# A two-layer encoder trunk with a mixture of experts on one core: gathering the tokens of two experts at once, the gate addition ahead of the routing, and another last combine

## The chip, the cores and the metric

The kernel runs on one core of a Trainium2 chip. TensorE (PE) multiplies, VectorE (DVE) and ScalarE (ACT) do the elementwise work, GpSimd (POOL) builds constants and issues a few DMAs, SyncE (SP) issues the weight DMAs. The metric is the device time of one launch in microseconds (us), the median of several runs.

## What is computed

Two layers over 256 tokens of width 1024, all in float32. Each layer normalizes, mixes along the sequence in four head groups and adds a gated residual; then comes a feed-forward part: a dense SwiGLU in layer 0, a top-2-of-8 mixture of SwiGLU experts in layer 1. A last RMSNorm ends it. The change lies in the mixture and behind it.

```python
D_MODEL, SEQ, DEPTH, D_FF, N_EXPERTS, TOP_K = 1024, 256, 2, 3584, 8, 2

def swiglu(h, w1, w3, w2):
    return (jax.nn.silu(h @ w1) * (h @ w3)) @ w2

def moe_ffn(h, router_w, router_b, w1, w3, w2):
    logits = h @ router_w + router_b
    top_v, top_i = lax.top_k(logits, TOP_K)
    combine = sum over k of one_hot(top_i) * softmax(top_v)
    y = jnp.zeros_like(h)
    for e in range(N_EXPERTS):
        y = y + combine[..., e:e + 1] * swiglu(h, w1[e], w3[e], w2[e])
    return y

h = modulate(rms_norm(x, norm_ffn[1]), sh2, sc2)
x = x + g2[:, None, :] * moe_ffn(h, ...)
return rms_norm(x, norm_final)
```

## The kernel before

Tokens lie in two tiles (`tt`) of 128 partitions. Each expert has 128 slots; its tokens are gathered into them by a product with a 0/1 matrix. `routing` computes logits on PE, picks the two best experts per token on DVE, and counts positions on PE; `dispatch_of` (L1706) writes `dispatch[token, slot]` for one expert, with one compare per token tile. `gather` (L1086) multiplies the normalized rows `xn` with it, in plain float32: 8 feature blocks of 128 by 2 token tiles, 128 columns each, 16 products an expert, which the trace records as 32. ACT copies the eight blocks out of PSUM with shift and scale (`fill_two`, L2095, into `x_slots`) and rounds them to `x_high` (`fill_high`); DVE subtracts for `x_low` (`fill_low`).

An expert reads 21 chunks of weights of 2 MB through a ring of six, in `MOE_ORDER`. Each chunk is two units. For each unit ACT rounds the weights to float32r (`w_high`, three buffers, L2121), DVE subtracts for the rest (`ring_low`, L1727), and PE does high x high, high x low and low x high (L1117 to L1119): 12 products of 512 columns. So ACT works three units ahead of PE at most (`used_at(r, m - HIGHS)`), and DVE behind ACT. In `two_experts` of ACT and DVE the place of every other step is written by hand behind a unit `m` of 42. PE's order is in `one_expert`: the next expert's gather stands between the units of `up(2, "w1")` and `up(2, "w3")`, that is ahead of unit 24. The result of an expert is gated (`y_gate`), split, spread back over the tokens by `combine` (8 products) and added to x (`sums`) in the course of the next expert; the last one's behind the loop. At the end `final` normalizes: ACT squares and takes roots, DVE divides and multiplies (L1841), SP stores.

A DMA that POOL issues loads the gate's bias row (L626) once the old one has been used; `gate(1, 1, ...)` adds two row sums to it on DVE (L1371), behind the routing. The number of tokens of the fullest expert, `most_i`, is loaded into a register by ACT and DVE ahead of their first steps for the experts (L2282, L1911); a second pass over the experts runs only where it is over 128, and the profiled execution has none.

The lines that the wait of the gate hangs on:

```python
            def gate(l, which, b):
                rep = 2 * l + which
                eng.wait_ge(s_gate, 16 * (rep + 1))
                eng.wait_ge(gate_t.sem, gate_t.at("sum", rep))
```

Of the kernel before, what the change touches and what calls it, by code (L numbers as in the profile page):

```python
# [6 lines left out]
P = 128  # L7
D = 1024
KB = D // P
T = 256  # L10
# [94 lines left out]
class Steps:  # L105
# [11 lines left out]
    def said(self, name):  # L117
# [86 lines left out]
        ("d0 d1").split(),  # L204
    "choice_v":
        ("c").split(),
# [5 lines left out]
        ("g0 g1").split(),  # L212
# [13 lines left out]
        ("la lb").split(),  # L226
    "fill_a":
        ("x0 x1 x2 x3 h0 x4 x5 x6 x7 h1").split(),
# [3 lines left out]
        ("y").split(),  # L232
    "end_v":
        ("rc0 o00 o01 rc1 o10 o11").split(),
    "end_a":
        ("table sq00 b0 sq10 b1 sq01 rt0 sq11 rt1").split(),
# [3 lines left out]
def hybrid_stream_block(nc, a, out):  # L240

    ctx = ExitStack()
    with ctx:
# [73 lines left out]
        x_slots = mb("x_slots", [P, KB, SLOTS])  # L317
# [3 lines left out]
        dispatch = mb("dispatch", [P, 2, TT, SLOTS])  # L321
        choice = mb("choice", [P, 2, 3, TT])
        chosen = mb("chosen", [P, 3, NE + 1, TT])
# [6 lines left out]
        y_high = mb("y_high", [P, D], F32R)  # L330
        y_low = mb("y_low", [P, D], F32R)
# [42 lines left out]
        disp_v, choice_v = steps("disp_v"), steps("choice_v")  # L374
        slot_v, slot_a, gather_t = steps("slot_v"), steps("slot_a"), steps("gather_t")
# [3 lines left out]
        end_v, end_a, half_t = steps("end_v"), steps("end_a"), steps("half_t")  # L379

# [144 lines left out]
        def last_sum(rep):  # L525

            return combined(rep, expert(rep, 0, NE))

        def combined(q, r):

            return r - 1 + q
# [15 lines left out]
        def _(eng):  # L547
# [44 lines left out]
            def store(rep):  # L592

                for tt, half in ((0, None), (1, 0), (1, 1)):
                    c = slice(0, D) if half is None else slice(half * W, (half + 1) * W)
                    eng.wait_ge(end_v.sem, end_v.at(f"o{tt}{1 if half is None else half}", rep))
                    eng.dma_start(out[0, tt * P:(tt + 1) * P, c], out_place(tt)[:, c]).then_inc(s_out, 16)
# [14 lines left out]
        def _(eng):  # L612
# [83 lines left out]
            for g, win in enumerate(WINDOWS):  # L696
# [29 lines left out]
               .then_inc(s_final, 16)  # L726

# [4 lines left out]
        def _(eng):  # L732
# [353 lines left out]
            def gather(b, u, first, name):  # L1086
# [5 lines left out]
                mark(ins.then_inc(gather_t.sem, 1), gather_t, name)  # L1092

            def experts(q):
                eng.wait_ge(disp_v.sem, disp_v.at("d1", q * NE))
                gather(bank[4], 0, 0, "g0")
                gather(bank[5], 0, 4, "g1")
# [11 lines left out]
                combine(combined(q, expert(q, 0, NE)))  # L1109

            def one_expert(q, g, u):
                r = expert(q, g, u)
                old = combined(q, r)
# [7 lines left out]
                def up(J, name, first, middle=None):  # L1121
# [4 lines left out]
                    for half in range(n_j):  # L1126
                        if half and middle:
                            middle()
                        if J == 0 and name == "w1":
                            eng.wait_ge(fill_v.sem, fill_v.at("lb" if half else "la", r))  # L1130
# [59 lines left out]
                def spread_turn():  # L1190
# [3 lines left out]
                    for tt in range(TT):  # L1194
                        ins = nc.tensor.transpose(bank[7][:, tt * P:(tt + 1) * P], dispatch[:, u, tt, :], ident)
# [26 lines left out]
                if not is_last(q, g, u):  # L1222
                    eng.wait_ge(disp_v.sem, disp_v.at("d1", r + 1))
                    eng.wait_ge(moe_v.sem, moe_v.at("al2", r))
                    gather(bank[6], (u + 1) % 2, 0, "g0")
                    eng.wait_ge(moe_v.sem, moe_v.at("al3", r))
                    gather(bank[7], (u + 1) % 2, 4, "g1")
                up(2, "w3", 2)
                down(2)
                down(3)  # L1230

                if is_last(q, g, u):
                    eng.wait_ge(moe_v.sem, moe_v.at("al3", r))
                else:
                    eng.wait_ge(fill_a.sem, fill_a.at("x3", r + 1))
                turn(4)
                if not is_last(q, g, u):
                    eng.wait_ge(fill_a.sem, fill_a.at("x7", r + 1))
# [12 lines left out]
            def combine(rep):  # L1251

                for tt, half, b in COMBINE:
# [4 lines left out]
                    if tt == 0:  # L1258
                        eng.wait_ge(comb_v.sem, comb_v.at(f"yl{half}", rep))
                    mark(mm(bank[b][:, :], spread[:, tt * P:(tt + 1) * P], y_low[:, half * W:(half + 1) * W],  # L1260
                            start=False, stop=True).then_inc(comb_t.sem, 1), comb_t, f"c{tt}{half}")

# [50 lines left out]
        def _(eng):  # L1313
# [336 lines left out]
            def routing():  # L1650
# [5 lines left out]
                ids = iota_f[:, 0:NE].unsqueeze(1).to_broadcast([P, TT, NE])  # L1656
                eng.wait_ge(route_t.sem, route_t.at("rows"))
# [24 lines left out]
                dispatch_of(0, 0, 0)  # L1682
# [13 lines left out]
                done_(nc.vector.memset(chosen[:, :, NE, :], 0.0).then_inc(route_v.sem, 1), "idle")  # L1696
                gate(1, 1, (bank[0], bank[1]))

            def fill_low(part, rep, u):

                eng.wait_ge(fill_a.sem, fill_a.at(f"h{part}", rep))
                k = 4 * part
                done(eng, tt_(x_low[:, u, k:k + 4, :], x_slots[:, k:k + 4, :], x_high[:, u, k:k + 4, :].bitcast(F32),
                              ALU.subtract).then_inc(fill_v.sem, 1), fill_v, "lb" if part else "la", rep)

            def dispatch_of(e, u, rep):  # L1706

                for tt in range(TT):
                    done(eng, ts_(dispatch[:, u, tt, :], iota_f, chosen[:, 0, e, tt:tt + 1],
                                  chosen[:, 1, e, tt:tt + 1], ALU.is_equal, ALU.mult).then_inc(disp_v.sem, 1),  # L1710
                         disp_v, f"d{tt}", rep)

            def dispatch_again(e, u, rep):
# [601 lines left out]
```

## Time and profile before

| | |
|---|---|
| median of 3 runs | 1590.28 us (1589.90 to 1591.51) |
| the profiled execution's own time | 1590.84 us |
| its span, first to last instruction | 1589.0 us |
| mean granted clock of TensorE | 0.988 of full speed |
| busy: PE, DVE, ACT | 98%, 82%, 62% |
| gathers, first and last start | 568.01 us, 1398.10 us |
| first expert's first product | 574.05 us |
| last store issued | 1584.68 us and 1.12 us for two |

The busy shares are of the whole span. The experts fill it from 574 us on. Ends of PE's instructions are modelled, so that neighbours overlap in the rows; the time that a product takes from the next is read from start to start.

### The profile page before, as it was taken

What the parts mean: (1) busy time and instruction counts of PE and PEld (TensorE: products, weight loads), DVE (VectorE), ACT (ScalarE), POOL (GpSimd) and SP (SyncE); (2) the same over time, 40 slices, a digit from 0 to 9 for tenths busy, and PEclk for the clock granted to TensorE, in tenths of its full rate; (3) what the DMA queues carried; (4) which work ended last, traced back from release to release, by engine and by line L of the source; (5) the groups of instructions that cost most, each with busy time, mean ns of one, the idle gap of its engine ahead of it and who ended that gap; (6) DMA issues with size and microseconds to landing.
All of it is one profiled execution on the core that took longest, in us unless ns stands there. A gap on an engine that the chain in (4) does not pass through costs nothing.

```text
span 1589.0 us, 19707 instructions
## 1 busy us (share of the span) xinstructions
PE 1560.7 (98%) x8037; PEld 1280.9 (81%) x8037; DVE 1308.5 (82%) x1185; ACT 978.7 (62%) x879; POOL 43.5 (3%) x116
## 2 busy tenths in 40 slices
PE   8999999999999989999999999999999999999997
PEld 6886789999888468888888888888888888888885
DVE  5888878888674559899799799899988989989987
ACT  2432433444444357777777777687787777677775
POOL 5300100000000000000000000000000000000000
PEclk8999999999999999999999999999999999999999
DMA  9845788887823269999999999899999999999990
GB/s 354 309 162 210 265 312 324 308 299 266 304 96 117 79 226 366 339 366 346 336 366 354 329 368 361 322 368 364 354 339 369 341 339 373 344 343 364 346 354 28
DMA packets 157142, 481.05 MB, mean 303 GB/s; under 512 B 4218, under 2 KB 6438, under 8 KB 157046
## 3 DMA queue, kind: packets, MB, share of 16 engines
q1 hardware_dynamic: 155120, 475.02, 80.9%
q0 software_dynamic: 1392, 3.58, 0.7%
q8 instruction: 65, 1.06, 0.3%
q10 hardware_dynamic: 534, 1.13, 0.2%
q14 instruction: 31, 0.25, 0.0%
HBM read 478.66 MB, written 1.05 MB: 302 GB/s over the span
## 4 chain that ended last, share of the span: by engine, by line
PE 92%; DVE 5%; DMA 1%; ACT 1%; issue 1%; DVEq 0%; ACTq 0%
PE bank L1119 20%; PE bank L1117 20%; PE bank L1118 19%; PE bank L813 6%; PE bank L1037 3%; PE bank L1039 3%; PE bank L1038 3%; PE bank L810 3%; PE bank L1090 2%; PE bank L1013 2%; PE bank L1014 2%; PE bank L1148 2%; PE bank L1015 2%; DMA ring<-in_w_mod_dram 1%; PE bank L998 1%; PE bank L747 1%
## 5 line engine op out<-in xcount | busy, mean ns | idle before, releaser
L1727 DVE TENSOR_TENSOR ring_low<-ring,w_high 128x2048 fp32r<-128x2048 f32 x336 | 766.9, 2291 | 116.1 <-ACT w_high L2121 108.8
L2121 ACT ACTIVATE w_high<-ring 128x2048 fp32r<-128x2048 f32 x336 | 646.4, 1924 | 240.7 <-PE bank L1119 230.8
L1117 PE MATMUL bank<-w_high,x_high 128*128 128x512 f32 x896 | 355.9, 397 | 2.2 <-issue 2.2
L1118 PE MATMUL bank<-ring_low,x_high 128*128 128x512 f32 x896 | 355.9, 397 | 0.0
L1119 PE MATMUL bank<-w_high,x_low 128*128 128x512 f32 x896 | 353.9, 395 | 0.0
L1117 PEld LDWEIGHTS bank<-w_high,x_high 128*128 128x128 f32 x896 | 169.1, 189 | 43.7 <-DVE ring_low L1727 2.6
L1119 PEld LDWEIGHTS bank<-w_high,x_low 128*128 128x128 f32 x896 | 168.5, 188 | 37.7
L1118 PEld LDWEIGHTS bank<-ring_low,x_high 128*128 128x128 f32 x896 | 168.8, 188 | 36.9
L2060 ACT ACTIVATE tmp_r<-ring 128x1024 fp32r<-128x1024 f32 x84 | 89.1, 1063 | 148.2 <-PE bank L1039 86.7
L1119 PE MATMUL bank<-w_high,act_low 128*128 128x512 f32 x448 | 178.0, 397 | 0.0
L1117 PE MATMUL bank<-w_high,act_high 128*128 128x512 f32 x448 | 177.1, 395 | 0.3 <-DVE ring_low L1727 0.3
L1118 PE MATMUL bank<-ring_low,act_high 128*128 128x512 f32 x448 | 174.1, 389 | 0.0
L1037 PE MATMUL bank<-h_high,tmp_r 128*128 128x256 f32 x448 | 126.8, 283 | 4.2 <-DVE ring_low L1612 3.0
L1612 DVE TENSOR_TENSOR ring_low<-ring,tmp_r 128x1024 fp32r<-128x1024 f32 x84 | 102.2, 1224 | 33.2 <-ACT tmp_r L2060 31.3
L1039 PE MATMUL bank<-h_low,tmp_r 128*128 128x256 f32 x448 | 126.5, 282 | 0.0
L1038 PE MATMUL bank<-h_high,ring_low 128*128 128x256 f32 x448 | 125.4, 280 | 0.0
L1118 PEld LDWEIGHTS bank<-ring_low,act_high 128*128 128x128 f32 x448 | 84.1, 188 | 20.3
L1119 PEld LDWEIGHTS bank<-w_high,act_low 128*128 128x128 f32 x448 | 84.1, 188 | 19.8
L1117 PEld LDWEIGHTS bank<-w_high,act_high 128*128 128x128 f32 x448 | 84.2, 188 | 18.7 <-DVE ring_low L1727 0.7
L813 PE MATMUL bank<-h_t,ring 128*128 128x256 f32 x384 | 91.8, 397 | 2.0 <-ACT h_t L1951 2.0
L1037 PEld LDWEIGHTS bank<-h_high,tmp_r 128*128 128x128 f32 x448 | 86.2, 192 | 5.6 <-DVE ring_low L1612 3.2
L813 PEld LDWEIGHTS bank<-h_t,ring 128*128 128x128 f32 x384 | 74.9, 198 | 15.5 <-issue 2.9
(330 smaller groups left out, 1705.9 us busy)
## 6 DMA issues: line engine op xcount, KB each, us to landing
ring<-in_moe_w_dram SPq DMA_DIRECT2D x168, 2048.0 KB, 7.9
ring<-in_w_mod_dram SPq DMA_DIRECT2D x23, 2048.0 KB, 10.9
ring<-in_ffn_w_dram SPq DMA_DIRECT2D x21, 2048.0 KB, 13.3
ring<-in_w_in_dram SPq DMA_DIRECT2D x8, 2048.0 KB, 18.6
ring<-in_w_out_dram SPq DMA_DIRECT2D x4, 2048.0 KB, 8.4
ring<-in_w_mod_dram SPq DMA_DIRECT2D x2, 1024.0 KB, 16.2
gate_row<-in_b_mod_dram POOLq DMA_DIRECT2D x4, 512.0 KB, 8.0
ring<-in_w_in_dram SPq DMA_DIRECT2D x2, 1024.0 KB, 11.5
```

The costliest lines, as they stand in the source:

```text
L810: ins = mm(b[:, i * G:(i + 1) * G], h_t[:, k, i * P:(i + 1) * P], w[:, k, off:off + G], start=k == 0, stop=k == KB - 1)
L813: ins = mm(b[:, i * T:(i + 1) * T], w[:, k, off + i * P:off + (i + 1) * P], h_t[:, k, :], start=k == 0, stop=k == KB - 1)
L1037: mm(o, w_h[:, k, :], h_high[:, k, :], start=k == 0, stop=False)
L1038: mm(o, w_l[:, k, :], h_high[:, k, :], start=False, stop=False)
L1039: ins = mm(o, w_h[:, k, :], h_low[:, k, :], start=False, stop=k == KB - 1)
L1117: mm(out_, x_h, w_h, start=first, stop=False)
L1118: mm(out_, x_h, w_l, start=False, stop=False)
L1119: return mm(out_, x_l, w_h, start=False, stop=last)
L1612: mark(tt_(quarter(ring_low, QUARTERS[m]), quarter(ring, QUARTERS[m]), quarter_high(m).bitcast(F32), ALU.subtract).then_inc(ffn_l.sem, 1), ...
L1727: tt_(moe_low(u, m // 2)[:, c], moe_slot(u, m // 2)[:, c], w_high[:, m % HIGHS, :].bitcast(F32), ALU.subtract).then_inc(low_made, 1)
L2060: mark(act(quarter_high(m), quarter(ring, QUARTERS[m]), ACT.Copy).then_inc(ffn_h.sem, 1), ffn_h, "q")
L2121: act(w_high[:, m % HIGHS, :], moe_slot(u, m // 2)[:, c], ACT.Copy).then_inc(high_made, 1)
```

## The change

1. **Gather.** `dispatch` holds both experts of a pair side by side, so that one product has 256 columns (two experts by 128 slots). The rows are split in two parts in float32r, `xn_high` (ACT, `token_high`) and `xn_low` (POOL, one subtraction per token tile), and each is multiplied: 8 blocks by 2 tiles by 2 parts, 32 products a pair. It is done ahead of the first expert, and in the second expert of a pair: half of it ahead of unit 24, half ahead of unit 28. `x_slots` has both experts' slots; its copies have 256 columns.
2. **Routing.** `gate(1, 1, ...)` stands ahead of the wait for the router's product. Four dispatch compares instead of two stand ahead of the first gather. ACT and DVE load `most_i` behind their first fills.
3. **End.** The last expert's result: the first half of the columns is split and spread as before; the second half is spread in one plain float32 product per token tile, without a split. In `final` DVE multiplies x by `norm_final` early for token tile 1, and ACT applies the root's reciprocal to it.
4. **Room.** `y_high` and `y_low` lie in `act_high` and `act_low`, `xn_low` in the dense FFN's `h_high`.

```diff
+        y_high = act_high[:, :, :].rearrange("p a n -> p (a n)")
+        y_low = act_low[:, :, :].rearrange("p a n -> p (a n)")
+        xn_high = mb("xn_high", [P, TT, D], F32R)
+        xn_low = h_high[:, :, :].rearrange("p (t b) c -> p t (b c)", t=TT)
...
+            eng.wait_ge(norm_t.sem, norm_t.at("t3", 3))        # POOL
+            for tt in range(TT):
+                eng.wait_ge(split_a.sem, split_a.at(f"x{tt}"))
+                done(eng, eng.tensor_tensor(xn_low[:, tt, :], xn[:, tt, :], xn_high[:, tt, :].bitcast(F32),
+                                            ALU.subtract).then_inc(split_v.sem, 1), split_v, f"x{tt}")
...
-                for k in range(4):
+                for k in (2 * n, 2 * n + 1):                   # PE, gather
                     for tt in range(TT):
-                        ins = mm(b[:, k * P:(k + 1) * P], xn[:, tt, (first + k) * P:(first + k + 1) * P],
-                                 dispatch[:, u, tt, :], start=tt == 0, stop=tt == TT - 1)
+                        for part in (xn_high, xn_low):
+                            ins = mm(b[:, k % 2 * T:(k % 2 + 1) * T], part[:, tt, k * P:(k + 1) * P],
+                                     dispatch[:, tt, :, :].rearrange("p u n -> p (u n)"),
+                                     start=tt == 0 and part is xn_high, stop=tt == TT - 1 and part is xn_low)
...
+                more = u == PAIR - 1 and not is_last(q, g, u)
+                eng.wait_ge(moe_v.sem, moe_v.at("al3", r))
+                if more:
+                    eng.wait_ge(disp_v.sem, disp_v.at("d11", after))
+                    gather(bank[6], 0)
+                    gather(bank[7], 1)
                 up(2, "w3", 2)
+                if more:
+                    eng.wait_ge(fill_a.sem, fill_a.at("x1", after))
+                    gather(bank[6], 2)
+                    eng.wait_ge(fill_a.sem, fill_a.at("x3", after))
+                    gather(bank[7], 3)
                 down(2)
...
+            def last_combine(q):
+                eng.wait_ge(last_a.sem, last_a.at("yh0", q))
+                for tt, half, b in COMBINE[0:2]:
+                    mm(bank[b][:, :], spread[:, tt * P:(tt + 1) * P], y_high[:, W:D], start=True, stop=False)
...
+                eng.wait_ge(last_v.sem, last_v.at("yg1", q))
+                for tt, half, b in COMBINE[2:4]:
+                    mark(mm(bank[b][:, :], spread[:, tt * P:(tt + 1) * P].bitcast(F32), act_m[:, 1, :],
+                            start=True, stop=True).then_inc(last_t.sem, 1), last_t, f"c{tt}1")
...
+                gate(1, 1, (bank[0], bank[1]))                 # DVE, routing
                 eng.wait_ge(route_t.sem, route_t.at("rows"))
...
-                        if m in (28, 29) and not last:         # ACT, two_experts
-                            fill_two(bank[6], 2 * (m - 28), r + 1)
...
+                        if m in (20, 28) and u == 0:
+                            fill_high((m - 20) // 8, now, 1)
+                        if m in (27, 28) and more:
+                            fill_two(bank[m - 21], m - 27, after)
+                        if m == 30 and more:
+                            fill_high(0, after, 0)
+                        if m in (31, 32) and more:
+                            fill_two(bank[m - 25], m - 29, after)
+                        if m == 33 and more:
+                            fill_high(1, after, 0)
```

On DVE, from the last normalization to the first steps of the routing (L1658 adds the router's bias to the logits), stood:

```order
L1379 TENSOR_SCALAR xn<-x,norm_s 128x1024
L1388 TENSOR_SCALAR h_t<-bank,mod_col 128x256 x4
L1658 TENSOR_SCALAR logits_t<-bank,router_bias 8x256
L1661 COPY route<-bank 128x16
L1665 TENSOR_REDUCE route_c<-route 128x2
L1666 TENSOR_TENSOR route<-route,route_c 128x16
```

and now stand:

```order
L1423 TENSOR_SCALAR xn<-x,norm_s 128x1024
L1432 TENSOR_SCALAR h_t<-bank,mod_col 128x256 x4
L1415 TENSOR_TENSOR gate_row<-bank,gate_row 128x512 x2
L1703 TENSOR_SCALAR logits_t<-bank,router_bias 8x256
L1706 COPY route<-bank 128x16
L1710 TENSOR_REDUCE route_c<-route 128x2
L1711 TENSOR_TENSOR route<-route,route_c 128x16
```

The two additions of the gate (L1415) have moved ahead of the logits; behind the routing they are gone. On ACT, between the routing's exponential and the first expert, stood:

```order
L2280 ACTIVATE route_c<-route_c 128x2
L2282 TENSOR_LOAD most_i
L2282 ISA x2
L2103 ACTIVATE x_slots<-bank,mod_col 128x128 x4
L2110 ACTIVATE x_high<-x_slots 128x512
L2103 ACTIVATE x_slots<-bank,mod_col 128x128 x4
L2110 ACTIVATE x_high<-x_slots 128x512
L2121 ACTIVATE w_high<-ring 128x2048 x4
```

and now stand:

```order
L2372 ACTIVATE route_c<-route_c 128x2
L2186 ACTIVATE x_slots<-bank,mod_col 128x256 x4
L2193 ACTIVATE x_high<-x_slots 128x512
L2186 ACTIVATE x_slots<-bank,mod_col 128x256 x4
L2193 ACTIVATE x_high<-x_slots 128x512
L2284 TENSOR_LOAD most_i
L2284 ISA x2
L2204 ACTIVATE w_high<-ring 128x2048 x4
```

The register load has moved behind the fills, and each copy has 256 columns. On ACT, in an expert that fills for the next (the second of a pair now), from unit 28 on, stood:

```order
L2121 ACTIVATE w_high<-ring 128x2048
L2103 ACTIVATE x_slots<-bank,mod_col 128x128 x2
L2121 ACTIVATE w_high<-ring 128x2048
L2103 ACTIVATE x_slots<-bank,mod_col 128x128 x2
L2121 ACTIVATE w_high<-ring 128x2048
L2110 ACTIVATE x_high<-x_slots 128x512
L2103 ACTIVATE x_slots<-bank,mod_col 128x128 x2
L2121 ACTIVATE w_high<-ring 128x2048
L2103 ACTIVATE x_slots<-bank,mod_col 128x128 x2
L2121 ACTIVATE w_high<-ring 128x2048
L2110 ACTIVATE x_high<-x_slots 128x512
L2121 ACTIVATE w_high<-ring 128x2048 x2
```

and now, from the silu behind unit 27 (L2230) on:

```order
L2230 ACTIVATE act_s<-bank 128x512
L2186 ACTIVATE x_slots<-bank,mod_col 128x256 x2
L2204 ACTIVATE w_high<-ring 128x2048
L2186 ACTIVATE x_slots<-bank,mod_col 128x256 x2
L2204 ACTIVATE w_high<-ring 128x2048 x2
L2193 ACTIVATE x_high<-x_slots 128x512
L2204 ACTIVATE w_high<-ring 128x2048
L2186 ACTIVATE x_slots<-bank,mod_col 128x256 x2
L2204 ACTIVATE w_high<-ring 128x2048
L2186 ACTIVATE x_slots<-bank,mod_col 128x256 x2
L2204 ACTIVATE w_high<-ring 128x2048
L2193 ACTIVATE x_high<-x_slots 128x512
```

The first copies come one unit earlier, the last rounding one unit later.

## Rows read from the trace of the kernel before

**Rows 1.** The page's part 4: engines on the chain that ended last
```profile
PE 92%; DVE 5%; DMA 1%; ACT 1%; issue 1%; DVEq 0%; ACTq 0%
```

**Rows 2.** Busy time in a stretch of the experts: us, then each engine, clock, DMA, GB/s
```profile
950.00:1075.00 125.00, 125.00 (x573) 102.29 (x572) 111.35 (x68) 93.42 (x70) 0.00 (x0) 1.00 0.95 351
```

**Rows 3.** Timeline of PE around gathers: start us, us, engine, line, operation, count
```profile
644.72 3.73 PE L1090 MATMUL bank<-dispatch,xn 128*128 128x128 f32 x32
...
648.21 0.48 PE L1117 MATMUL bank<-w_high,x_high 128*128 128x512 f32 x1
648.52 0.40 PE L1118 MATMUL bank<-ring_low,x_high 128*128 128x512 f32 x1
...
649.91 0.40 PE L1118 MATMUL bank<-ring_low,x_high 128*128 128x512 f32 x1
...
1398.10 3.73 PE L1090 MATMUL bank<-dispatch,xn 128*128 128x128 f32 x32
```

**Rows 4.** Timeline of PE and page part 5, dense FFN: products of 256 columns
```profile
311.03 0.28 PE L1037 MATMUL bank<-h_high,tmp_r 128*128 128x256 f32 x1
...
316.92 0.28 PE L1039 MATMUL bank<-h_low,tmp_r 128*128 128x256 f32 x1
...
L1037 PEld LDWEIGHTS bank<-h_high,tmp_r 128*128 128x128 f32 x448 | 86.2, 192 | 5.6 <-DVE ring_low L1612 3.2
```

**Rows 5.** The page's part 5: busy us, mean ns, idle before, releaser
```profile
L1727 DVE TENSOR_TENSOR ring_low<-ring,w_high 128x2048 fp32r<-128x2048 f32 x336 | 766.9, 2291 | 116.1 <-ACT w_high L2121 108.8
L2121 ACT ACTIVATE w_high<-ring 128x2048 fp32r<-128x2048 f32 x336 | 646.4, 1924 | 240.7 <-PE bank L1119 230.8
```

**Rows 6.** Timeline from routing to the first expert, DVE, ACT and PE
```profile
557.41 2.35 ACT L1951 ACTIVATE h_t<-bank,mod_col 128x256 f32<-128x256 f32 x4 [1.67 <-PE bank L781]
557.62 2.28 DVE L1388 TENSOR_SCALAR h_t<-bank,mod_col 128x256 f32<-128x256 f32 x4 [0.82 <-PE bank L781]
...
562.44 0.47 DVE L1658 TENSOR_SCALAR logits_t<-bank,router_bias 8x256 f32<-8x256 f32 x1 [2.54 <-PE bank L1068]
...
567.23 0.73 DVE L1709 TENSOR_SCALAR dispatch<-consts,chosen 128x128 f32<-128x128 f32 x2
...
568.01 3.84 PE L1090 MATMUL bank<-dispatch,xn 128*128 128x128 f32 x32 [0.65 <-DVE dispatch L1709]
...
569.95 1.42 DVE L1371 TENSOR_TENSOR gate_row<-bank,gate_row 128x512 f32<-128x512 f32 x2
570.64 1.93 ACT L2103 ACTIVATE x_slots<-bank,mod_col 128x128 f32<-128x128 f32 x4 [2.85 <-PE bank L1090]
...
574.05 0.47 PE L1117 MATMUL bank<-w_high,x_high 128*128 128x512 f32 x1 [2.20 <-issue]
```

**Rows 7.** Timeline of POOL, and the DMA issues: KB, us from issue to landing
```profile
554.89 0.81 POOL L626 DMA_DIRECT2D gate_row<-in_b_mod_dram  x1 [123.75 <-DVE x L1402]
...
gate_row<-in_b_mod_dram POOLq DMA_DIRECT2D x1, 512.0 KB, 8.2
```

**Rows 8.** Timeline of PE and busy time (granted clock behind POOL) after the routing
```profile
577.64 0.53 PE L1117 MATMUL bank<-w_high,x_high 128*128 128x512 f32 x1
...
576.00:577.00 1.00, 1.00 (x4) 0.81 (x3) 0.65 (x1) 0.00 (x0) 0.00 (x0) 0.50 0.00 0
```

**Rows 9.** Groups by line on POOL: busy us, mean ns, idle before
```profile
L706 POOL TENSOR_TENSOR band_a<-band_a,consts 128x128 f32<-128x128 f32 x4 | 2.2, 558 | 0.3
```

**Rows 10.** Timeline of the end, and of PE's plain float32 products at 512 columns
```profile
529.47 13.90 PE L998 MATMUL bank<-ring,xn 128*128 128x512 f32 x32
...
1575.53 0.69 DVE L1736 TENSOR_TENSOR act_m<-bank,gate_row 128x512 f32<-128x512 f32 x1 [0.69 <-PE bank L1119]
...
1577.77 3.11 DVE L1751 SCALAR_TENSOR_TENSOR x<-bank,chosen,x 128x512 f32<-128x512 f32 x4
...
1578.62 0.63 ACT L2211 ACTIVATE x_slots<-x 128x512 f32<-128x512 f32 x1 [0.16 <-DVE x L1751]
...
1584.68 1.12 SPq L597 DMA_DIRECT2D out_dram<-act_m  x2
```

More of the change, by code:

```diff
@@ L203 @@
     "disp_v":
-        ("d0 d1").split(),
+        ("d00 d10 d01 d11").split(),
     "choice_v":
-        ("c").split(),
+        ("keep c0 c1").split(),
+    "split_a":
+        ("x0 x1").split(),
+    "split_v":
+        ("x0 x1").split(),
     "slot_v":
@@ L523, in expert, with combined, pair @@
             return q * NE + g * PAIR + u
[L525 to L531, printed above, removed]
+        def combined(r):
+            return r - 1
+        def pair(q, g):
+            return q * (NE // PAIR) + g
         def is_first(q, g, u):
@@ L1681, in routing @@
                       "ch0")
[L1682 removed]
+                for tt in range(TT):
+                    dispatch_of(tt, 0)
                 eng.wait_ge(route_a.sem, route_a.at("exp"))
@@ L1720, in dispatch_again @@
+            def dispatch_again(tt, rep):
+                for u in range(PAIR):
+                    done(eng, ts_(dispatch[:, tt, u, :], iota_f, choice[:, u, 0, tt:tt + 1],
                                   choice[:, u, 1, tt:tt + 1], ALU.is_equal, ALU.mult).then_inc(disp_v.sem, 1),
-                         disp_v, f"d{tt}", rep)
+                         disp_v, f"d{u}{tt}", rep)
             def low(r, u, m):
@@ L1757, in two_experts @@
                     r = expert(q, g, u)
-                    old = combined(q, r)
+                    old = combined(r)
                     first, last = is_first(q, g, u), is_last(q, g, u)
-                    old_weight = choice[:, (u + 1) % 2, 2, :] if q else chosen[:, 2, r - 1, :] if r else None
+                    old_weight = choice[:, 0 if u else PAIR, 2, :] if q else chosen[:, 2, r - 1, :] if r else None
+                    more = u == PAIR - 1 and not last
+                    now, after = pair(q, g), pair(q, g) + 1
                     def product(j):
@@ L1802, in two_experts @@
                             product(m - 26)
-                        if m in (33, 35) and not last:
-                            fill_low((m - 33) // 2, r + 1, (u + 1) % 2)
+                        if m in (33, 35) and more:
+                            fill_low((m - 33) // 2, after, 0)
                         if m == 34:
@@ L2132, in two_experts @@
                     r = expert(q, g, u)
-                    old = combined(q, r)
+                    old = combined(r)
                     first, last = is_first(q, g, u), is_last(q, g, u)
+                    more = u == PAIR - 1 and not last
+                    now, after = pair(q, g), pair(q, g) + 1
                     def act_highs(j):
@@ L2220, in final @@
                                   scale=1.0 / D).then_inc(end_a.sem, 1), end_a, f"rt{tt}", rep)
+                eng.wait_ge(end_v.sem, end_v.at("rc1", rep))
+                for half in range(2):
+                    o = out_place(1)[:, half * W:(half + 1) * W]
+                    done(eng, act(o, o, ACT.Copy, scale=norm_s[:, 2, 1:2]).then_inc(end_a.sem, 1), end_a, f"o1{half}", rep)
             def layer_constants():
```

239 lines of the change are left out of this document (134 added, 105 removed).

## The prediction

> **What bounds the kernel now.** I read the chain that ended last first: 92% of it is PE [rows 1], so the question is what PE does and when it waits. The experts take the span from 574 us on. In a stretch of 125 us there PE is busy for 125.00, DVE for 111.35 and ACT for 93.42, at full granted clock, with the DMA engines at 0.95 and 351 GB/s [rows 2]. The ends of PE's rows are modelled, so I check by counting. Two gathers six experts apart start at 644.72 and 1398.10, 125.56 us an expert [rows 3]. Products of 512 columns come (649.91 - 648.52) / 6 = 0.2317 us apart [rows 3]; an expert has 504, and 8 in the combine: 118.6 us. The gather takes 3.5, and its 30 transposes the rest. Nothing is left for a wait: the loop is bound by PE's own work, and each product less is time less, as long as ACT and DVE keep up.
>
> **The gather in the loop.** An expert's gather runs from 644.72 to 648.21, 3.49 us, and the first product behind it takes 0.31 us to the next instead of 0.23 [rows 3]: 3.57 us. Seven of the eight stand inside the experts: 7 x 3.57 = 25.0 us go. What comes is 3 gathers of 32 products, float32r, 256 columns, stationary 128x128. The dense FFN has just these: 51 of them from 311.03 to 316.92, 50 steps of 0.118 us [rows 4]. That is 3.77 us a pair, 11.3 us in all. **Loop: -13.7 us.** The lower end of a product's price is that 0.118; the upper end is a load of 0.19 us that isn't hidden plus 0.28 us, both in [rows 4], and I take the first, since those rows have the same shape and type.
>
> **What hides it must still hide.** The w_high buffers let ACT start on unit m+3 when PE has ended unit m, so the chain of ACT (1.92 us) and DVE (2.29 us) [rows 5] must fit in two units of PE, 2 x 12 x 0.2317 = 5.56 us. 1.35 us is left for hand-overs and for steps in between. A gather gave both engines 3.5 us more, once an expert. Now the first expert of a pair has none, and takes 122.0 us; DVE's work in it, 111.35 x 125.56/125 = 111.8 us with two subtractions for x_low as before, is 92% of it. DVE waits for ACT for 108.8 us over 336 units, 0.32 us a unit, and ACT for PE for 230.8 us, 0.69 us a unit [rows 5], so neither is at its end. Stepping through units 20 to 36 with these durations, every one is ready before PE wants it: the two turns ahead of unit 20 give 0.9 us, and the fills of that expert are gone from ACT. In the second expert of a pair the copies have 256 columns, 2.35 / 4 = 0.59 us each against 1.93 / 4 = 0.48 [rows 6], but 8 a pair for 16: ACT gains. The gather's halves wait for x1 and x3, which ACT has ready some 4 us before PE gets there. The two dispatch compares at unit 16, 0.73 us [rows 6], fit into DVE's waits. I take 0 us for all of that; its ends are 0 and the 4 x 3.57 = 14.3 us that the experts without a gather could give back.
>
> **The routing.** The gate's additions move ahead of the logits. DVE is free from 559.9 to 562.44, and the additions take 1.42 us [rows 6], so they would fit. But they wait for the bias row, which POOL issues at 554.89 and which lands 8.2 us later, at 563.1 [rows 7]. So they end at 564.5 and the logits start then instead of at 562.44: +2.1 us on the routing's path. Behind the routing the additions cost nothing, since DVE then waits for ACT anyway: what is removed there brings nothing. Ends of this term: 0 (row there in time) and +3.5. Two compares more ahead of the gather: +0.73 [rows 6]. The first gather then starts at 568.01 + 2.8 = 570.8 us.
>
> From the gather's start to the first expert's first product it is 6.04 us now: ACT's copies start 2.63 us after it [rows 6], because half the gather is 1.9 us, and because ACT loads most_i before. Now two groups of blocks are waited for apart, the first after 8 products, 0.94 us and 0.2 for its end: 1.1 us. The four copies take 0.42 us longer. So 6.04 - 1.5 + 0.4 = 4.9, and PE starts at 575.75, **+1.7 us**. The rest of the gather, 3.77 us, ends before that.
>
> The clock: after PE's idle 2.2 us at 571.9 the granted clock is 0.50 at 576 to 577 us, and nine products from 574.05 to 577.64 take 3.59 us instead of 2.09 [rows 6, 8]: 1.5 us lost. With the gather packed up to 1.1 us before the first expert I expect this fall to go. But with late logits PE idles for 2.8 us at 562.3, and can fall there or ahead of the gather, which costs about 1 us in the filler products ahead of the position counts or in a slow gather. So -1.5 and +0.8. **Routing in all: +1.7 - 1.5 + 0.8 = +1.0 us**, ends -0.5 and +4.
>
> The split of xn costs ACT two copies of 128x1024 in waits (one ahead of its first h block, one behind the last, when it idles until 566), and POOL two subtractions. The nearest row of POOL is 0.558 us for 128 columns [rows 9]; eight times that is 4.5 us, two are 9.0. They start at about 558.2 with the last transposes and end at 567.2 at the worst, before the gather at 570.8: 0 us.
>
> A rule speaks against that. While POOL subtracts, DVE's operations with two inputs in SBUF could be held up; no row here shows the two at once. The Trainium skill, SBUF — State Buffer, section Who interferes with whom, says that such a DVE operation and a GpSimd operation that reads SBUF share a port as an exclusive lock, and that the second one blocks until the first is done. By it the routing's small steps would wait for POOL, and the sum would be 1579; without it they wait for nothing. It is a rival below.
>
> **The end.** Now DVE gates the second half at 1575.53 for 0.69 us; ACT's and DVE's split follow, and the sums start only at 1577.77, 3.11 us for four [rows 10]. In the change the first half's spread is done by then, so the sums start right behind the gate, at 1576.25: -1.5 us. The second half's plain products take 13.90 / 16 = 0.87 us each [rows 10]; they end at 1577.3 and 1578.2, where the third and fourth sums are due at 1577.8 and 1578.6: hidden. ACT's squares, 1578.62 now, follow at 1577.1. Behind its last root DVE now multiplies one tile after the other; in the change ACT scales tile 1 while DVE does tile 0, 0.5 us more. The last of the stores (1584.68, two in 1.12 us) is issued some 1.8 us earlier. **End: -1.8 us**, ends -1.0 and -2.4.
>
> **The sum.** 1590.84 (the profiled execution's own time) - 13.7 + 1.0 - 1.8 = 1576.3 us. The median of the runs is 0.6 us below that execution; between the two I write 1576.0.
>
> **Rivals.**
> - *ACT and DVE don't keep up in the experts without a gather.* For: 1.35 us of room, and DVE at 92%. Against: DVE's waits for ACT of 0.32 us a unit show room that can be used. Giving back half of 14.3 us it would be 1583. Chance 0.14.
> - *POOL's subtractions hold DVE up in the routing:* from 567.2 - 565.5 = 1.7 us to one subtraction of 4.5 us; with some 2.7, 1579. For: they are as late as the gate. Against: most of their time falls where DVE waits for the bias row. 0.07.
> - *The weights come no faster.* Then the loop keeps 125.56 us an expert and only the ends change: 1590.0. For: DMA engines at 0.95. Against: of ACT's 240.7 us of waits 230.8 are for PE [rows 5], and only 351 x 125.56 / 122.0 = 361 GB/s are asked for. 0.04.
> - *Slower: the load of the stationary operand doesn't hide behind 256 columns.* Each product of the gathers would take 0.19 + 0.28 = 0.47 us [rows 4], a pair 15.0 instead of 3.77, four of them +45: 1621. It decides from 0.118 + 14.5 / 128 = 0.23 us a product, where the gain is zero. For: the load's 0.19 us is longer than the step of 0.118 it would hide behind. Against: in the 50 steps it does. 0.03.
> - Better than forecast (no fall of the clock, bias row early), below 1573.5: 0.04.
>
> The forecast, 1573.5 to 1578.5, has 0.68. The range 1573.5 to 1581.5 adds the second rival and the better part of the first. Faster by over 0.2% (3.2 us, about what can be told from no change) 0.91; within it 0.05, for the third rival and the far end of the first; slower 0.04.
>
> **What will show it.** Gather products 0.118 us apart; pairs of experts 247.8 us long; no waits of PE for ring_low between 580 and 1560; the gate's additions starting at 563.1 and the logits behind them; the first expert's product at 575.8 at full clock; DVE's sums in the end straight behind the gate. A pair over 250 us would prove the loop's term wrong, logits at 562.4 the routing's.

## The result and the profile after

The changed kernel takes 1583.6 us (median of 5 runs, 1581.09 to 1585.52) against 1591.51 for the kernel before on the same chip (5 runs): a ratio of 0.9949, 95% interval 0.9938 to 0.9960. It is faster, but by 8 us where 14.5 were forecast, and the time lies outside the range of 1573.5 to 1581.5. A second series gave 1582.92 against 1592.96 and a ratio of 0.9932 (0.9919 to 0.9945), so 10.8 us by the ratio, and outside the range too. Gains and losses in us against the kernel before are worked out from the ratios; two versions of one series are compared by their medians. The profiled execution is one of 1583.6 us, with a span of 1581.9.

The experts first. This is the page of the kernel after, the chain and three groups (line, operation, tiles | busy us, mean ns | idle before, releaser):

```profile
PE 93%; DVE 5%; DMA 1%; ACT 1%; issue 0%; POOL 0%; DVEq 0%; ACTq 0%; POOLq 0%
...
L1780 DVE TENSOR_TENSOR ring_low<-ring,w_high 128x2048 fp32r<-128x2048 f32 x336 | 768.1, 2292 | 100.8 <-ACT w_high L2204 93.8
L2204 ACT ACTIVATE w_high<-ring 128x2048 fp32r<-128x2048 f32 x336 | 646.2, 1925 | 238.6 <-PE bank L1145 229.3
L1143 PE MATMUL bank<-w_high,x_high 128*128 128x512 f32 x896 | 355.7, 397 | 0.8 <-issue 0.8
```

PE's timeline around gathers of the kernel after (start us, us, engine, line, operation):

```profile
772.90 0.28 PE L1114 MATMUL bank<-dispatch,xn_high 128*128 128x256 f32 x1
...
774.67 0.28 PE L1114 MATMUL bank<-dispatch,h_high 128*128 128x256 f32 x1
774.79 0.39 PE L1143 MATMUL bank<-w_high,x_high 128*128 128x512 f32 x1
...
1020.90 0.28 PE L1114 MATMUL bank<-dispatch,xn_high 128*128 128x256 f32 x1
```

Beside [rows 3]: sixteen products take 774.79 - 772.90 = 1.89 us, 0.118 each, and a pair of experts 1020.90 - 772.90 = 248.0 us, where two experts took 251.1. Beside [rows 5]: DVE and ACT take as long for a unit as before, and DVE waits for ACT 15 us less in all, which is where the room came from. PE's products with `w_high` and `x_high` have 0.8 us of idle time ahead of them in the whole span, the wait ahead of the first expert.

The routing, beside [rows 6], is the timeline of DVE and PE from the gate's additions on:

```profile
557.41 0.69 DVE L1446 TENSOR_TENSOR x<-x,h_t 128x512 f32<-128x512 f32 x1
...
566.07 1.42 DVE L1415 TENSOR_TENSOR gate_row<-bank,gate_row 128x512 f32<-128x512 f32 x2 [2.66 <-DMA gate_row<-in_b_mod_dram]
567.52 0.47 DVE L1703 TENSOR_SCALAR logits_t<-bank,router_bias 8x256 f32<-8x256 f32 x1
568.05 0.28 PE L1095 MATMUL bank<-consts,logits_t 8*128 8x8 f32 x2 [2.24 <-DVE logits_t L1703]
568.26 4.54 PE L787 MATMUL bank<-consts 128*128 128x512 f32 x6
...
571.33 0.18 DVE L1721 COPY chosen<-route 128x16 f32<-128x16 f32 x1
572.64 0.28 PE L1101 MATMUL bank<-route,consts 128*128 128x8 f32 x2
...
573.48 0.17 DVE L1724 COPY chosen<-bank 128x16 f32<-128x16 f32 x1 [1.97 <-PE bank L1103]
573.69 1.49 DVE L1755 TENSOR_SCALAR dispatch<-consts,chosen 128x128 fp32r<-128x128 f32 x4
575.24 0.39 PE L1114 MATMUL bank<-dispatch,xn_high 128*128 128x256 f32 x1 [1.42 <-DVE dispatch L1755]
...
581.62 0.47 PE L1143 MATMUL bank<-w_high,x_high 128*128 128x512 f32 x1 [0.81 <-issue]
```

The additions wait for the bias row, and the logits with them. Then three filler products (plain float32, results unused, to keep PE busy; six in the trace's count) take 4.54 us. They hold up the position products, which count the tokens' places in their experts: their input is there at 571.1, ahead of the copy at 571.33, and they start at 572.64. PE's windows in that place (us, busy of PE, PEld, DVE, ACT, POOL, granted clock, DMA share, GB/s), beside [rows 8]:

```profile
569.00:570.00 1.00, 1.00 (x3) 0.48 (x2) 0.83 (x6) 0.00 (x0) 0.00 (x0) 0.50 1.00 410
...
573.00:574.00 1.00, 0.82 (x8) 0.73 (x7) 0.49 (x2) 0.00 (x0) 0.00 (x0) 1.00 0.00 0
576.00:577.00 1.00, 1.00 (x7) 1.00 (x6) 0.84 (x5) 0.00 (x0) 0.00 (x0) 0.50 0.00 0
...
579.00:580.00 1.00, 1.00 (x11) 1.00 (x10) 0.00 (x0) 0.97 (x2) 0.00 (x0) 1.00 0.00 0
```

The clock falls to its lower level (1.2 of 2.4 GHz) twice, once under the fillers and once under the gather, whose products are 0.21 us apart until 579.0.

The end of the kernel after, beside [rows 10]:

```profile
1568.84 0.69 DVE L1897 TENSOR_TENSOR act_m<-bank,gate_row 128x512 f32<-128x512 f32 x1 [0.69 <-PE bank L1145]
1569.57 3.11 DVE L1902 SCALAR_TENSOR_TENSOR x<-bank,chosen,x 128x512 f32<-128x512 f32 x4
1569.59 1.98 PE L1304 MATMUL bank<-act_m,spread 128*128 128x512 f32 x4
...
1572.71 1.42 DVE L1909 TENSOR_TENSOR act_m<-x,final_row 128x512 f32<-128x512 f32 x2
...
1574.16 0.16 DVE L1913 RECIPROCAL norm_s<-norm_s 128x1 f32<-128x1 f32 x1
...
1575.68 1.48 ACT L2312 ACTIVATE act_m<-act_m,norm_s 128x512 f32<-128x512 f32 x2 [0.98 <-DVE norm_s L1913]
1576.12 0.36 SPq L614 DMA_DIRECT2D out_dram<-act_s  x1
1576.52 1.26 SPq L614 DMA_DIRECT2D out_dram<-act_m  x2
```

The sums stand straight behind the gate, as forecast. But two multiplications of 1.42 us together now stand between the sums and the first reciprocal.

**One table for all runs.** A is the start of the last residual addition ahead of the routing. "Gather" and "first" are the first gather and the first expert's first product, counted from A. "Loop" goes from there to the last combine's first product, "end" from that to the end of the span. All in us, of one profiled execution each; "falls" are the moments between 560 and 580 us at which the granted clock falls to 0.50. "Second profile" is the same kernel profiled again.

```
kernel                  A       gather  first   loop     end    falls
before                  553.91  14.10   20.14   1001.21  13.74  574.5
before, second profile  555.69  14.10   20.14    999.75  13.82  none
before, gate early      557.16  17.40   23.45    999.54  13.65  568.7
after                   557.41  17.83   24.21    986.95  13.33  568.7, 575.5
after, second profile   556.23  17.87   24.37    987.18  13.22  567.4, 574.2
after, gate back        556.16  14.84   21.35    986.86  12.93  571.1
after, row early        555.95  14.84   20.35    987.09  12.91  572.1
after, fillers          554.47  16.65   22.78    987.05  13.20  571.7
after, old final        556.07  16.47   22.94    987.08  12.31  572.7
after, other layout     554.55  16.32   22.73    987.00  12.82  570.7
gather in pairs alone   554.79  14.84   20.07    986.72  13.82  none
back_old                554.56  14.85   20.07    986.78  12.19  none
back_old_fill           556.28  14.84   20.07    986.78  12.17  none
back_old_fill_4k        556.83  14.84   20.08    986.86  12.23  none
```

From before to after: 3.5 (A) + 4.1 (first) - 14.3 (loop) - 0.4 (end) = -7.1, the difference of the spans. Between the two second profiles, of which before's has no fall here: +0.5 + 4.2 - 12.6 - 0.6 = -8.5, for spans that differ by 8.4.

### The profile page after: what moved, and what is told of

It reads as the page before. It is cut to its first block, busy times and chain, and to the rows that moved or that the text cites. A ratio compares the mean times of both kernels' runs of the same rounds, so it can differ in the third digit from the quotient of the medians.

```text
span 1581.9 us, 19404 instructions
## 1 busy us (share of the span) xinstructions
PE 1553.9 (98%) x7909; PEld 1271.3 (80%) x7909; DVE 1309.0 (83%) x1184; ACT 971.3 (61%) x850; POOL 48.9 (3%) x118
## 4 chain that ended last, share of the span: by engine, by line
PE 93%; DVE 5%; DMA 1%; ACT 1%; issue 0%; POOL 0%; DVEq 0%; ACTq 0%; POOLq 0%
PE bank L1143 20%; PE bank L1144 20%; PE bank L1145 19%; PE bank L836 6%; PE bank L1062 3%; PE bank L1060 3%; PE bank L1061 3%; PE bank L833 3%; PE bank L1036 2%; PE bank L1037 2%; PE bank L1038 2%; PE bank L1174 2%; PE bank L787 1%; PE bank L1114 1%; PE bank L1021 1%; PE bank L770 1%
## 6 DMA issues: line engine op xcount, KB each, us to landing
ring<-in_w_mod_dram SPq DMA_DIRECT2D x23, 2048.0 KB, 10.8
```

## The experiments

**What belongs to the change, and what to the execution: both kernels again, unchanged.**

> The changed kernel once more, not altered, to see what chance does to the part ahead of the change. Its profiled execution reached the last residual addition 3.5 us later than the kernel before (557.41 for 553.91 us). If that was chance (another fall of TensorE's clock at some 135 us), this profile reaches it anywhere from 553 to 558 us, and the parts behind it stay: 24.2 us to the first expert's product, 987.0 in the experts, 13.3 at the end. If the change itself costs it (other places in memory), it is again 3 us or more above 553.9. Time 1583 us, ratio 0.995.

> The kernel before once more, not altered, for a second profile. Theory: its first profiled execution was an early one of its kind, so now the last residual addition comes later than 553.9 us, at 555.5 to 557.5, as in four of five profiles of the changed kinds (556.0 to 557.4), with 20.1 us to the first expert's product, 1001.2 in the experts and 13.7 at the end again. Rival: the change costs the part ahead of it 2 us; then 553.9 us comes again.

The kernel after again has two falls and its first product 24.37 us behind A, so the late first product is no accident of one profile. The kernel before took 1591.15 us; its second profile has no fall after the routing, its first expert runs at full clock, and its loop is 1.5 us shorter for it. That fall, which I credited the change with removing, wasn't in every execution. A moves over 3.5 us: 553.9 to 557.2 in the kernels with before's loop, and 554.5 to 557.4 in those with after's, though no computation ahead of it is changed. The profile that I summed from had the earliest A of all fourteen.

**The gate early, alone, in the kernel before.**

```
+                gate(1, 1, (bank[0], bank[1]))
                 eng.wait_ge(route_t.sem, route_t.at("rows"))
                 done_(ts_(logits_t[:, :], bank[2][0:NE, 0:T], router_bias[:, 0:1], None, ALU.add)...
                 ...
-                gate(1, 1, (bank[0], bank[1]))
```

> The kernel before with one part of the change alone: the gate's additions ahead of the logits. Theory: the landing of the bias row holds the logits for 1.6 us, and the idle TensorE adds a fall of its clock, of which the fillers behind the logits pay 1.7 us more: the first expert's product comes 22 to 23.5 us behind the residual instead of 20.1, time 1.5 to 3.5 us above before, ratio 1.001 to 1.002. Rival: in the kernel before the additions cost nothing, since the first gather is waited for by nothing else; then 20.1 stays.

1595.36 us against 1591.04, ratio 1.0023 (1.0013 to 1.0033). By itself this edit makes the kernel slower by 3.7 us (2.1 to 5.3). Timeline of DVE and PE of that kernel:

```profile
566.16 1.42 DVE L1371 TENSOR_TENSOR gate_row<-bank,gate_row 128x512 f32<-128x512 f32 x2 [3.00 <-DMA gate_row<-in_b_mod_dram]
567.61 0.47 DVE L1659 TENSOR_SCALAR logits_t<-bank,router_bias 8x256 f32<-8x256 f32 x1
568.14 0.29 PE L1072 MATMUL bank<-consts,logits_t 8*128 8x8 f32 x2 [2.55 <-DVE logits_t L1659]
568.35 4.54 PE L764 MATMUL bank<-consts 128*128 128x512 f32 x6
```

The same wait and the same 4.54 us of fillers as in the kernel after, with no subtraction on POOL: so POOL isn't what makes them.

**The gate's additions put back behind the routing in the kernel after** (the same lines, the other way round).

> The changed kernel with the gate's two additions where they stood, behind the routing. Theory: the early additions wait for the bias row until 566.07, hold the logits for 1.6 us, and TensorE's idling of 2.2 us there lets its clock fall, which stretches the filler products and the first gather by some 3 us. Then the logits come 8.5 us behind the last residual addition instead of 10.1, the first expert's product 19.8 us instead of 24.2, and the time is 1579 us, 4.4 less. Rival: the routing is late because POOL's subtractions hold DVE; then the logits' start moves by 1.6 us and nothing behind it. Rival: the clock would fall anyhow, since the gather is thin; then the gain is 1.6 to 2 us.

1578.67 us, ratio 0.9906 (0.9892 to 0.9919), 4.2 us less than the kernel after in the same series. The gather starts 14.84 us behind A for 17.87, and the first product comes at 21.35 for 24.37. The 19.8 us that were expected for it didn't come, since one fall of the clock stayed: at 571.1, under the gather.

**The gate early, but its bias row loaded 16 us sooner** (issued 14.9 us ahead of A for 1.0 us behind it) into a buffer that is free then, with a semaphore of its own.

```
-            eng.wait_ge(res_v.sem, res_v.at("r7", 2))
+            eng.wait_ge(mix_v.sem, mix_v.at("yd1", 1))
             load_gate(1, "g2")
+            eng.wait_ge(res_v.sem, res_v.at("r7", 2))
```

> The changed kernel with the gate's additions left ahead of the logits, but their bias row loaded some 18 us earlier into a buffer of its own. Theory: only the landing of the row made the move dear; the additions then fit into DVE's wait of 2.5 us for the router's product, the logits come 8.5 us behind the last residual addition, the first product 19.8, and the time equals gate_back's within 0.5 us, 1579. Rival: the additions themselves hold the logits up, by their 1.42 us; then the logits come 9.9 us behind, and half of gate_back's gain is missing.

1578.98 us, ratio 0.9914 (0.9902 to 0.9927). The additions stand ahead of the logits as in the change, and cost nothing: the logits start 8.51 us behind A, as with the gate back, for 10.1 in the kernel after. It is the row's landing that costs, not the place of the additions.

**Two more filler products ahead of PE's wait for the logits.** They are there only to keep PE busy; the trace counts four.

```
                 mark(ins.then_inc(route_t.sem, 1), route_t, "rows")
+                keep_clock(bank[5], steady, 2)
                 eng.wait_ge(route_v.sem, route_v.at("lgt", 0))
```

> The changed kernel with two more filler products (plain float32, 512 columns, results unused) on TensorE ahead of its wait for the logits. They change nothing on DVE, so the logits stay 10.1 us behind the last residual addition. Theory: the idle stretch of 2.2 us there let the clock fall; with 1.7 us of it filled the granted clock stays at 1.0, the three fillers behind the logits take 2.84 us instead of 4.54, and the first expert's product comes 21.5 us behind the residual instead of 24.2; time 1581. Rival: the clock falls because of the thin router and position products whatever the fillers do; then 24.2 stays.

1579.56 us, ratio 0.9915 (0.9902 to 0.9928), 3.4 us less than the kernel after. Timeline of PE:

```profile
562.80 1.98 PE L787 MATMUL bank<-consts 128*128 128x512 f32 x4
565.31 0.29 PE L1096 MATMUL bank<-consts,logits_t 8*128 8x8 f32 x2 [0.52 <-DVE logits_t L1704]
565.52 2.84 PE L787 MATMUL bank<-consts 128*128 128x512 f32 x6
```

PE idles 0.52 us for 2.24, and the next fillers run at full clock in 2.84 us. The logits are as late as before, so this part of the price was the clock alone: the gather starts 1.2 us earlier behind A, and the first product 1.6 us. One fall stayed, at 571.7, and the first product came at 22.78, not at the 21.5 that were expected. The ratio promises more than the stages show; 1.8 us of the profile's gain is an earlier A.

**The old final in the kernel after.**

```
     "end_v":
-        ("f0 f1 rc0 o00 rc1 o01").split(),
+        ("rc0 o00 o01 rc1 o10 o11").split(),
     "end_a":
-        ("table sq00 b0 sq10 b1 sq01 rt0 sq11 rt1 o10 o11").split(),
+        ("table sq00 b0 sq10 b1 sq01 rt0 sq11 rt1").split(),
```

> The changed kernel with the last combine as changed, but the old final: DVE multiplies both token tiles, ACT scales none, x isn't multiplied by norm_final ahead. Theory: the new final brings nothing, because its two early multiplications (1.42 us) stand on DVE ahead of the first reciprocal; then the last store is issued 9.2 us and the span ends 13.3 us behind the combine's start, as in the changed kernel within 0.2. Rival (the prediction's step): ACT and DVE side by side save 0.5 us; then 9.7 and 13.8.

One run, 1580.11 us. The end takes 12.31 us, and 12.2 in the three kernels of the kind back_old below, which have the same last combine and the same old final. The six profiles with the new final have 12.8 to 13.3 (the table), so the new final costs 0.5 to 1.1 us of the end. The timeline of DVE and SP here, for comparison with the kernel after:

```profile
1567.08 3.11 DVE L1899 SCALAR_TENSOR_TENSOR x<-bank,chosen,x 128x512 f32<-128x512 f32 x4
1571.27 0.17 DVE L1906 RECIPROCAL norm_s<-norm_s 128x1 f32<-128x1 f32 x1 [1.07 <-ACT norm_s L2301]
...
1574.02 1.12 SPq L611 DMA_DIRECT2D out_dram<-act_m  x2
```

From the sums' start to the first reciprocal it is 4.19 us here and 4.59 there; to the last stores' issue 6.94 and 6.95. So the new final issues them no earlier. The rest is the landing: from the start of the last store's issue to the end of the span it is 3.6 us here (1574.81 to 1578.40) and 4.7 there (1577.18 to 1581.88). It is 4.1 to 4.7 us in all six profiles with the new final and 3.4 to 3.6 in all eight with the old one, so the later landing goes with the new final. There the last two stores follow the first one's start by 0.40 us, here by 0.98; that they land later for this is likely, but no run tries it alone.

**Where the pair's buffers lie** (x_slots ahead of x_high).

> The changed kernel with x_slots placed ahead of x_high in memory, nothing else. In the changed kernel products of an expert's first units come 0.2336 us apart, in the kernel before 0.2311, some 0.2 us an expert, and a pair takes 248.0 us where the count of products gives 247.7. Theory: which part of memory the operands lie in decides that; then the spacing differs here (a pair takes 247.6 to 247.8 us or over 248.2). Rival: it comes from what ACT and DVE do beside these products; then 247.98 us again.

One run, 1578.79 us; pairs of 248.01 us, as before. What is missing in the loop isn't in the buffers' places.

**The gather in pairs alone:** the gate behind the routing, the old last combine, the old final.

```
-                last_combine(q)
+                combine(combined(expert(q, 0, NE)), 1)
```

> The gather in pairs alone: gate, last combine and final as in the kernel before (the last result's split parts only lie in the other halves of their buffers). Theory: the loop alone gives 12.7 us (987.0 in the experts against 999.7 in the profiles without a fall of the clock there), the first expert's product comes 20.3 to 21.4 us behind the residual for 20.1, and the end stays at 13.8: 11.5 to 12.5 us below before, 1579.5, ratio 0.9925. Rival: the end gives part of what is measured; then this kernel is equal to gate_back (1578.7) within 0.3.

1578.13 us, ratio 0.9918 (0.9901 to 0.9935): 13.0 us, nearly all of it the loop's.

**The same with the new last combine:** the gather in pairs, the gate behind the routing, the old final.

> The gather in pairs and the new last combine, with the gate behind the routing and the old final. Theory: the combine's early sums give 1.3 us, the new final gave nothing or cost up to 1 us: last store issued 9.1 us and the span ended 12.3 to 13.0 us behind the combine's start, 0.3 to 1 us below gate_back: 1578.0, ratio 0.990. Rival: the new final is worth 0.5 us; then it is 0.5 above gate_back and the end takes 13.8.

1576.1 us, ratio 0.9907 (0.9890 to 0.9925), the lowest median of all. The end takes 12.19 us for 13.82: the new last combine, whose second half is spread in plain float32 without a split, is worth 1.6 us in the profiled executions. The times alone don't settle it, as the intervals of the two ratios overlap. Its end and its routing:

```profile
1561.68 0.69 DVE L1894 TENSOR_TENSOR act_m<-bank,gate_row 128x512 f32<-128x512 f32 x1 [0.69 <-PE bank L1142]
1562.41 3.11 DVE L1899 SCALAR_TENSOR_TENSOR x<-bank,chosen,x 128x512 f32<-128x512 f32 x4
1562.43 1.98 PE L1301 MATMUL bank<-act_m,spread 128*128 128x512 f32 x4
...
1566.59 0.16 DVE L1906 RECIPROCAL norm_s<-norm_s 128x1 f32<-128x1 f32 x1 [1.08 <-ACT norm_s L2301]
```

```profile
563.07 0.47 DVE L1699 TENSOR_SCALAR logits_t<-bank,router_bias 8x256 f32<-8x256 f32 x1 [2.51 <-PE bank L1088]
...
569.41 0.39 PE L1111 MATMUL bank<-dispatch,xn_high 128*128 128x256 f32 x1 [1.42 <-DVE dispatch L1752]
569.63 0.28 PE L1111 MATMUL bank<-dispatch,h_high 128*128 128x256 f32 x1
```

**One filler ahead of the first gather, and with it a shift of 4 KB.**

```
                 mark(ins.then_inc(route_t.sem, 1), route_t, "most")
+                keep_clock(bank[7], steady, 1)
```

> back_old with one filler product (0.87 us, result unused) on TensorE ahead of its wait for the first gather's matrix. Theory: TensorE's thin work before the gather lets the granted clock fall as the gather runs (0.51 in gate_back), which makes 32 products take 6 us for 3.8; with the filler the clock stays, the first product comes 20.0 us behind the residual instead of 21.35, and the time falls by 1.3 us, to 1576.7. Rival: the fall only comes later, in the experts; then the first product comes at 20.0 but the loop takes 988.5, and the time is back_old's. Rival: one filler is too little; then 21.35 stays.

> back_old_fill with act_s ahead of x_high in memory, which moves x_high, x_low and w_high by 4 KB a partition. In the kernel before x_high lay 4 KB further than in the changed one; moving it 8 KB (layout) changed nothing. Theory: the 0.2336 us between products of an expert's first units, for 0.2311 before, comes from the place of x_high and w_high in steps of 4 KB; then the loop takes 986.0 instead of 987.0. Rival: the place has no part in it; then 987.0 stays.

1577.6 us, ratio 0.9909 (0.9893 to 0.9925), and 1577.45 us, 0.9910 (0.9895 to 0.9926). No difference: PE idles 0.46 us for 1.42 ahead of the gather, and there was no fall to prevent in the kernel without the filler either; the expectation had taken gate back's fall for this kernel's. The loop is 986.8 us in all three, so the shift does nothing.

## Why the prediction was wrong

The failed step is "Routing in all: +1.7 - 1.5 + 0.8 = +1.0 us". Its mechanism was named, its sizes were wrong: between the second profiles the routing costs 4.2 us. The forecast was -14.5 us in all, and these two profiles differ by -8.4. Of the 6.1 us between them, 3.2 are the routing's, 1.1 the loop's, 1.2 the end's, and 0.5 an A that came later by chance.

- *The wait.* Forecast: additions behind the row's landing, logits +2.1 us. Measured +1.6. Right, and shown to be the landing (row early).
- *The dispatch compares and the half gather.* In the kernels with the gate back and no fall (gather in pairs alone, back_old) the gather starts 0.74 us later than before (forecast 0.73), and the first product comes 5.23 us behind it (forecast 4.9). Added to the late logits that makes 14.10 + 0.74 + 1.6 + 5.23 = 21.7, or +1.5; forecast +1.7. Right.
- *The clock, +0.8.* Measured 24.21 - 21.7 = 2.5 us: 17.83 - 16.44 = 1.4 on the position products behind slow fillers, and 6.38 - 5.23 = 1.15 on the slow gather. The prediction names both places, but as alternatives of about 1 us each, and takes 0.8 for them. The kernel after shows both, in both profiles, and each cost more. Versions of it with one fall have their first product 20.35 to 22.94 us behind A, and those without 20.07 to 20.08.
- *The clock, -1.5.* The prediction took a fall in one profiled execution for a property of the kernel; the second profile has none to take away.

The gather's term: -13.7 forecast, -12.4 to -13.0 measured between the undisturbed loops (999.75 and 999.54 against 986.7 to 987.2), 0.7 to 1.3 short. A pair takes 248.0 us for 247.8, and there are four. The 0.118 us, the hidden load and the room on DVE and ACT hold. What is missing shows in the spacing of the 512-column products. Here is one stretch in PE's timeline, first of the kernel after, then of the kernel before in its second profile:

```profile
828.25 0.40 PE L1144 MATMUL bank<-ring_low,x_high 128*128 128x512 f32 x1
...
850.19 0.39 PE L1145 MATMUL bank<-w_high,x_low 128*128 128x512 f32 x1
```

```profile
825.41 0.40 PE L1118 MATMUL bank<-ring_low,x_high 128*128 128x512 f32 x1
...
847.14 0.40 PE L1119 MATMUL bank<-w_high,x_low 128*128 128x512 f32 x1
```

Both are 94 steps: 21.94 / 94 = 0.2334 us and 21.73 / 94 = 0.2312. The experts that I measured have one such stretch each, 8 x 0.21 = 1.7 us in all, and other groups differ either way, so part is given back. Why it is slower stays open; the buffers' places were tried twice (other layout, back_old_fill_4k), and aren't it.

The end: -1.8 forecast, -0.4 and -0.6 measured. The last combine gave 1.6, against 1.5 expected. For the new final the working says 0.5 more, of which its total of 1.8 takes in only 0.3; measured, it costs 0.5 to 1.1. Left out were the two multiplications ahead of the first reciprocal, of whose 1.42 us 0.4 don't hide behind ACT's root, and the stores' landing was taken as fixed.

Then there is the profile that was summed from. Its A was 1.8 us earlier than in before's second profile, while its fall cost 1.5. By luck the two nearly cancel, so its span was ordinary; but the prediction took the fall's 1.5 us back and kept the early A.

The rivals: ACT and DVE kept up, the weights came at the pace, and the stationary load is hidden. POOL's subtractions took 2.35 us each, half of the 4.5 us that the prediction scaled up from 128 columns, and the second one ran under the gate's additions:

```profile
561.54 2.35 POOL L748 TENSOR_TENSOR h_high<-xn,xn_high 128x1024 fp32r<-128x1024 f32 x1 [1.81 <-PE bank L804]
564.48 2.35 POOL L748 TENSOR_TENSOR h_high<-xn,xn_high 128x1024 fp32r<-128x1024 f32 x1 [0.59 <-ACT xn_high L2037]
```

The additions took 1.42 us, as in [rows 6] without it. They have one input in SBUF and one in PSUM, so the port rule of the Trainium skill (SBUF — State Buffer, Who interferes with whom), which speaks of two inputs in SBUF, isn't tested by it; no run here shows such an operation beside POOL's subtractions. The prediction says that no row shows the two at once, but the trace of the kernel before has some, far ahead of the change, and they agree with that rule. Here are POOL and DVE there:

```profile
46.98 5.55 DVE L1339 SCALAR_TENSOR_TENSOR mod_acc<-ring,c_act,mod_acc 128x512 f32<-128x512 f32 x7
...
51.13 0.85 POOL L706 TENSOR_TENSOR band_a<-band_a,consts 128x128 f32<-128x128 f32 x1
...
53.13 0.46 POOL L706 TENSOR_TENSOR band_b<-band_b,consts 128x128 f32<-128x128 f32 x1
```

Beside DVE's operations on `ring` and `mod_acc`, both in SBUF, POOL's addition takes 0.85 us; once they are over it takes 0.46. All fourteen profiles have eight such additions: the 22 that overlap an operation of DVE of this kind take 0.85 to 0.87 us, the 90 others 0.45 to 0.49. So the effect that the rival fears is real on this chip, here at POOL's cost. It stayed away in the routing, whose operations with two inputs in SBUF came behind both subtractions. The 0.85 is also one of the four in the mean of 0.558 us in [rows 9], which the 4.5 us were scaled from.

## What to carry to other kernels

When an idle engine's work is moved ahead of a critical step, ask of every input when it lands, not only whether the engine is free: 1.42 us of additions, made to wait for a DMA's landing ahead of the logits, cost 3.7 us by themselves and 4.2 in the whole change. Load the row earlier, or leave the work where it was. Before crediting a change with the end of a fall of the clock, take a second profile of the kernel before. In the kernel after the longer wait came with two falls, and each was paid by whatever filler or gather ran under it. Sum each small edit of a change by itself: two of four here lost time, and without them the change gives 14.8 us in place of 8.1 (10.8 in the second series). The early gate's loss shows in the times. The new final's shows only in the profiled executions: gate back, which has it, has a ratio of 0.9906 and back_old, which doesn't, 0.9907.

## What the runs showed of the hardware

The clock's falls to 0.50 come and go between executions of one kernel, also far ahead of the change: from 100 to 145 us the mean granted clock is 0.96 in before's profile, 1.00 in its second profile, and 0.92 in both of the kernel after. In the kernel after they start 2.9 and 9.7 us after the start of PE's wait for the logits, 2.24 us long. But PE idled as long there in the old final (2.26) and the other layout (2.10), and the clock fell only 8.3 and 7.7 us after the wait's start, at 572.7 and 570.7; the 1.42 us of idle time ahead of the gather are in versions with a fall and without. What sets the moment isn't settled here. Float32r products of 256 columns with a new 128x128 stationary each ran 0.118 us apart although the load's record is 0.19 us, in the loop as in the FFN.
